# Turning token tiles in the second model: scaled tiles and a transpose, or one product with a diagonal

## The chip, the cores and the metric

The kernel runs on one core of a Trainium2 chip. The metric is the device time of one execution, in microseconds (us). A core has TensorE for matrix products (its records are PE, its weight loads PEld), VectorE (DVE), ScalarE (ACT) and GpSimd (POOL), which run side by side and wait for one another by semaphores; SyncE (SP) issues most transfers.

## The reference

Two models run one after the other on 256 tokens of width 1024. The change touches the second, of four blocks, whose core is this:

```python
def second_block(x, c, positions, ada_w, ada_b, norm_g, ffn_w1, ffn_w2, ...):
    for i in range(DEPTH_2):                                    # 4 blocks
        h = modulate_2(rms_norm_2(x, norm_g[i, 0]), sh_a, sc_a) # "norm"
        y = mixer(h)                        # i = 0, 3: mla; 1: stick_breaking; 2: retention
        x = x + g_a[:, None, :] * rms_norm_2(y, norm_g[i, 1])
        h = modulate_2(rms_norm_2(x, norm_g[i, 2]), sh_f, sc_f) # "fnorm"
        y = jnp.square(jax.nn.relu(h @ ffn_w1[i])) @ ffn_w2[i]
        x = x + g_f[:, None, :] * rms_norm_2(y, norm_g[i, 3])
    return x

def rms_norm_2(x, g):
    y = xf * lax.rsqrt(jnp.mean(xf * xf, axis=-1, keepdims=True) + EPS)
    return (y * g).astype(x.dtype)
```

So there are eight norms of the residual x, one ahead of each mixer and one ahead of each feed-forward stage (FFN). Everything is float32.

## The kernel before, in words

The residual x of the second model lies with tokens on the 128 partitions: two token tiles t = 0, 1, each 1024 wide, handled in halves of 512 (`h_tok(t, half)` in the tensor hT). The dense products want it the other way round, with the 1024 features on the partitions, in eight pieces k of 128. Between the two lies a **turn**, `turn_pe` (L1084): it both scales each token by its root 1/sqrt(mean square + eps) and transposes. There are eight turns, named b0_norm, b0_fnorm, and so on to b3_fnorm.

How a turn comes about:

- ScalarE squares the halves of x with a running sum (`square_act`, L959) and makes the root of a token tile from it by a logarithm and an exponential (`rms_act`, L967 and L970); VectorE supplies one small half sum to it (`half_dve`, L1019).
- VectorE writes, for each t, a 128x128 matrix with the roots on the diagonal: the identity times the column of roots (`diag_dve`, L1042).
- TensorE multiplies each 128x128 piece of x by this diagonal (L1094), 8 pieces for t = 0 and 8 for t = 1. The product is the transposed and scaled piece. Piece k goes to bank 4 + k // 2, at column 256 (k % 2) + 128 t, so a bank is full only when both token tiles are in it, and the banks fill in order during t = 1.
- ScalarE reads the banks with scale and bias of the modulation (`scaled_act`, L1132), 8 pieces of 128x256. In the blocks with an mla mixer (0 and 3) the norm turn is read by ScalarE for k = 0 to 3 and by VectorE for k = 4 to 7 (L2906).
- Except there, the pieces are split into a high and a low part, on VectorE (L1153, L1162) and ScalarE (L1142), and every weight tile of 1024 columns is split too, by ScalarE (L2427 in the FFN, L873 elsewhere) and VectorE (L3096, L877). TensorE then makes three products for each pair of pieces (L2032, L940; L2025 and L2028 in block 3). In the mla blocks TensorE multiplies the float32 pieces as they are (L1777).

The order on each engine is written out by hand. In the FFN of blocks 0 to 2 ScalarE has, behind the last root, two copies of a row from the banks (L1168, for the modulation of the next block), then the first weight tile (L2427), then L1132. In block 3 the two copies are missing; in the norm turns of blocks 1 and 2 the first weight tile is L873. VectorE has its half of the first weight tile (L3096 or L877) behind the diagonals. Ahead of the FFN, TensorE clears four banks (L1996) between the turn and the first product. At block 0 x comes from the first model through banks: TensorE transposes it (L2062), ScalarE squares it there and VectorE copies it to hT (L3146). GpSimd clears one area at the start of block 3 (L3228), as soon as the last half of x is there.

Of the kernel before, what the change touches and what calls it, by code (L numbers as in the profile page):

```python
# [19 lines left out]
ALU = mybir.AluOpType  # L20
# [3 lines left out]
P = 128  # L24
# [230 lines left out]
def block_program(nc, a, out, LAST=8):  # L255

    with ExitStack() as ctx:
# [376 lines left out]
        cond_row = region(W + 2048, [D])  # L634
        dots = small[:, 12:24]
        spill = region(18432 + 2560, [2, 512])
        diag = region(18432 + 3584, [TC, P])

        def two(v):
            return v.rearrange("p (a n) -> p a n", a=2)  # L640
# [2 lines left out]

            return hT[:, 4 * t + 2 * half:4 * t + 2 * half + 2, N:2 * N]

        def h_piece(t, k):
            return hT[:, 4 * t + k // 2, N + (k % 2) * P:N + (k % 2) * P + P]

        def gp_row(which, half):
            return uT[:, 4 * which + 2 * half:4 * which + 2 * half + 2, 0:N]  # L650
# [10 lines left out]

        def counters():
            return {"y_hi": 0, "sq": 0, "rs": 0, "u": 0, "t": 0, "sq_hist": [], "used": 0, "split": 0, "tok_sq": 0, "ms": 0,
                    "h_tok": 0, "diag": 0, "u_even": 0, "u_hi_act": 0, "u_hi_dve": 0}

        def stat_act(act, c, chunks, fill, width, rows=P):

# [312 lines left out]
        def h_square(act, c, half, t):  # L980
# [2 lines left out]
            act.wait_ge(S("h_tok"), c["h_tok"])  # L983
            square_act(act, c, h_tok(t, half), 16, half, t)

        def h_act(act, c):

            for half, t in BY_TOKENS:
                h_square(act, c, half, t)
                if half:  # L990
                    rms_act(act, c, 16, t)

        def down_act(act, c, name, norm):

            fs = [tok_fill(name, half, t) for half, t in BY_TOKENS]
            y_act(act, c, fs[0], 0, 0)
            y_act(act, c, fs[1], 1, 0)
            y_act(act, c, fs[2], 0, 1)
            if norm:
                h_square(act, c, 0, 0)  # L1000
                h_square(act, c, 1, 0)
            y_act(act, c, fs[3], 1, 1)
            if norm:
                rms_act(act, c, 16, 0)
                h_square(act, c, 0, 1)
                h_square(act, c, 1, 1)
                rms_act(act, c, 16, 1)

        def square_wait(dve, c, n=1):
            c["tok_sq"] += n  # L1010
            dve.wait_ge(S("tok_sq"), c["tok_sq"])

        def rms_wait(dve, c):
            c["ms"] += 1
            dve.wait_ge(S("tok_rs"), c["ms"])
# [19 lines left out]
                                           stat8[:, 12 + t:13 + t], h_tok(t, half), ALU.mult, ALU.add)\  # L1035
                .then_inc(S("h_tok"), 1)

        def diag_dve(dve, c):

            for t in range(TC):  # L1040
                rms_wait(dve, c)
                nc.vector.tensor_scalar(diag[:, t, :], ident, stat8[:, 28 + t:29 + t], None, ALU.mult)\  # L1042
                    .then_inc(S("diag"), 1)

        def post_dve(dve, c, i, which, name):

            rms_wait(dve, c)
            h_dve(dve, name, 0, 0)
            h_dve(dve, name, 1, 0)
            y_dve(dve, c, i, which, tok_fill(name, 1, 1), 1, 1)  # L1050
            rms_wait(dve, c)
            h_dve(dve, name, 0, 1)
            square_wait(dve, c)
            half_dve(16, 0)
            h_dve(dve, name, 1, 1)
            square_wait(dve, c, 2)
            half_dve(16, 1)
            c["tok_sq"] += 1
            diag_dve(dve, c)

        def down_dve(dve, c, i, name, norm, extra):

            y_dve(dve, c, i, 1, tok_fill(name, 0, 0), 0, 0)
            y_dve(dve, c, i, 1, tok_fill(name, 1, 0), 1, 0)
            rms_wait(dve, c)
            h_dve(dve, name, 0, 0)
            h_dve(dve, name, 1, 0)
            y_dve(dve, c, i, 1, tok_fill(name, 0, 1), 0, 1)
            if norm:
                extra()  # L1070
                square_wait(dve, c)
                half_dve(16, 0)
                c["tok_sq"] += 1
            y_dve(dve, c, i, 1, tok_fill(name, 1, 1), 1, 1)
            rms_wait(dve, c)
            h_dve(dve, name, 0, 1)
            h_dve(dve, name, 1, 1)
            if norm:
                square_wait(dve, c)
                half_dve(16, 1)  # L1080
                c["tok_sq"] += 1
                diag_dve(dve, c)

        def turn_pe(pe, c, name):  # L1084

            for t in range(TC):
                c["diag"] += 1
                pe.wait_ge(S("diag"), c["diag"])
                for k in range(KC):
                    f = plan[name][k // 2]  # L1090
                    o = (k % 2) * N + t * P
                    if t == 0 and k % 2 == 0:
                        f.open(pe)
                    mm = nc.tensor.matmul(PS[:, f.bank, o:o + P], h_piece(t, k), diag[:, t, :], start=True, stop=True)  # L1094
                    if t == TC - 1 and k % 2:
                        mm.then_inc(f.full.sem, 1)

        def cond_row_pe(pe, name):

# [975 lines left out]
        def _(act):  # L2075
# [377 lines left out]
            for half, t in BY_HALF:  # L2453
                f = tok_fill("entry", half, t)
                f.full.wait(act)
                square_act(act, c, PS[:, f.bank, :], 16, half, t)
                if half:
                    rms_act(act, c, 16, t)
            for i, kind in enumerate(KINDS):
                p = f"b{i}_"  # L2460
                if i:
# [18 lines left out]
        def _(dve):  # L2480
# [662 lines left out]
            for half, t in BY_HALF:  # L3143
# [2 lines left out]
                V_.tensor_copy(h_tok(t, half), two(PS[:, f.bank, :])).then_inc(f.free.sem, 1)  # L3146
                if half == 0:
                    half_dve(16, t)
            diag_dve(dve, c)
            for i, kind in enumerate(KINDS):  # L3150
                p = f"b{i}_"
                {"mla": mla_dve, "stick": stick_dve, "ret": ret_dve}[kind](i)
# [96 lines left out]
```

## Time and profile before

| what | value |
|---|---|
| device time, median of 3 runs | 2900.12 us (2898.72 to 2900.56) |
| profiled execution | span 2896.6 us, 3.5 us under the median for what lies around the span |
| busy: PE, PEld, DVE, ACT, POOL | 90%, 59%, 46%, 33%, 1% |
| chain that ended last | PE 72%, DMA 19%, DVE 4%, ACT 3%, issue 2% |
| mean granted clock of TensorE, 1500 us to the end | 0.97 of full |

The span is one profiled execution, from its first to its last instruction. The chain is followed back from the last instruction to what released it. The transfers of the chain belong to the experts of the first model, ahead of 1500 us. In the rows an arrow reads "written from": `banks<-arena,hT` writes the banks from arena and hT. "x32" counts records; a float32 product of 128x128 by 128x128 is two records, a transpose one. A time in brackets is the idle time ahead and who ended it. A granted clock of 1.00 is 2.4 GHz, 0.50 is 1.2 GHz.

### The profile page before, as it was taken

The numbers are of one execution on the slowest core, as the hardware profiler recorded it, in microseconds if no ns is written. First come the engines' busy times: TensorE is split into PE (matmuls) and PEld (weight loads), VectorE is DVE, ScalarE is ACT, GpSimd is POOL, SyncE is SP. The second block draws the span as 40 slices with busy tenths as digits, with TensorE's granted clock in tenths as the row PEclk, the third lists the DMA queues.
The fourth block names the chain that finished last, engine by engine and source line by source line (L and its number), as shares of the span: only waits on it lengthen the run. The fifth ranks groups of instructions, "written<-read, shape, count | busy, mean of one in ns | idle before, by whom it ended". The sixth has DMA issues, their size and how long they took to land.

```text
span 2896.6 us, 34037 instructions
## 1 busy us (share of the span) xinstructions
PE 2609.4 (90%) x13004; PEld 1714.1 (59%) x13004; DVE 1336.6 (46%) x2308; ACT 961.9 (33%) x1782; POOL 39.3 (1%) x51
## 2 busy tenths in 40 slices
PE   8999878787889888877779899999999999999999
PEld 3436423222465543222245789878988988985787
DVE  1764300001266520000025687567887458865676
ACT  3124210101121320000013555556555446544443
POOL 0010000000000000000000000000000000000000
PEclk9999999999999999999999999989999999999999
DMA  8674499999945459999991486515866427852242
GB/s 362 278 306 192 203 428 429 428 429 429 428 193 224 168 231 429 428 428 429 428 394 63 164 340 251 236 59 217 322 263 256 172 113 269 343 212 88 83 178 102
DMA packets 59492, 796.13 MB, mean 275 GB/s; under 512 B 8636, under 2 KB 9916, under 8 KB 10748
## 3 DMA queue, kind: packets, MB, share of 16 engines
q1 hardware_dynamic: 55664, 790.13, 66.8%
q10 hardware_dynamic: 3724, 4.59, 0.5%
q8 instruction: 68, 1.11, 0.2%
q14 instruction: 36, 0.29, 0.0%
HBM read 793.64 MB, written 1.05 MB: 274 GB/s over the span
## 4 chain that ended last, share of the span: by engine, by line
PE 72%; DMA 19%; DVE 4%; ACT 3%; issue 2%; SPq 0%; ACTq 0%; DVEq 0%; POOL 0%; POOLq 0%
PE banks L2008 12%; PE banks L2032 9%; PE banks L1504 8%; DMA ring<-in_t_gate 7%; PE banks L925 6%; DMA ring<-in_t_up 6%; PE banks L810 5%; PE banks L940 5%; DMA ring<-in_t_down 4%; PE banks L1520 3%; DMA arena<-in_t_gate 3%; PE banks L2025 2%; PE banks L1379 2%; PE banks L1573 2%; PE banks L797 2%
## 5 line engine op out<-in xcount | busy, mean ns | idle before, releaser
L1504 PE MATMUL banks<-ring,arena 128*64 128x512 f32 x1920 | 475.3, 619 | 100.9 <-DMA ring<-in_t_up 54.8
L1504 PEld LDWEIGHTS banks<-ring,arena 128*64 128x64 f32 x1920 | 162.3, 143 | 389.1 <-issue 345.4
L2633 DVE TENSOR_TENSOR arena<-arena,banks 128x512 f32<-128x512 f32 x32 | 22.0, 687 | 795.2 <-PE banks L1504 795.2
L3096 DVE TENSOR_TENSOR ring_lo<-ring,w_hi 128x1024 fp32r<-128x1024 f32 x256 | 313.3, 1225 | 133.9 <-ACT w_hi L2427 131.7
L2427 ACT CAST w_hi<-ring 128x1024 fp32r<-128x1024 f32 x256 | 268.4, 1055 | 314.9 <-PE banks L2008 166.3
L2032 PE MATMUL banks<-u_pair,w_hi 128*128 128x256 f32 x1536 | 278.8, 284 | 3.9 <-DVE ring_lo L3096 3.3
L2140 ACT COPY arena<-banks 32x512 f32 x96 | 55.3, 576 | 608.3 <-PE banks L1520 607.5
L2032 PEld LDWEIGHTS banks<-u_pair,w_hi 128*128 128x128 f32 x1536 | 240.1, 192 | 6.7 <-issue 3.9
L1520 PE MATMUL banks<-ring,arena 128*64 128x512 f32 x896 | 206.9, 616 | 28.4 <-DMA ring<-in_t_down 15.7
L2032 PE MATMUL banks<-u_pair,ring_lo 128*128 128x256 f32 x768 | 217.3, 283 | 0.0
L2008 PE MATMUL banks<-w_hi,ffn_h_hi 128*128 128x512 f32 x512 | 200.9, 392 | 0.0
L2008 PE MATMUL banks<-ring_lo,ffn_h_hi 128*128 128x512 f32 x512 | 199.4, 390 | 0.0
L2008 PE MATMUL banks<-w_hi,ffn_h_lo 128*128 128x512 f32 x512 | 199.3, 389 | 0.0
L1168 ACT COPY arena<-banks 128x256 f32<-128x256 f32 (+3 forms) x242 | 102.5, 443 | 231.0 <-PE banks L810 107.8
L3106 DVE SCALAR_TENSOR_TENSOR ring<-ring,arena 128x1024 f32<-128x1024 f32 x144 | 174.6, 1219 | 0.0
L1520 PEld LDWEIGHTS banks<-ring,arena 128*64 128x64 f32 x896 | 70.0, 141 | 147.3 <-issue 128.1
L2032 PEld LDWEIGHTS banks<-u_pair,ring_lo 128*128 128x128 f32 x768 | 147.3, 192 | 0.0
L810 PE MATMUL banks<-arena,ring 128*128 128x512 f32 (+1 forms) x384 | 140.4, 527 | 0.0
L810 PEld LDWEIGHTS banks<-arena,ring 128*128 128x128 f32 x384 | 73.7, 193 | 64.3 <-issue 60.6
L940 PE MATMUL banks<-uT_r,ring_lo 128*128 128x256 f32 x384 | 108.6, 283 | 0.0
L2008 PEld LDWEIGHTS banks<-w_hi,ffn_h_lo 128*128 128x128 f32 x512 | 96.1, 188 | 20.2
L2008 PEld LDWEIGHTS banks<-w_hi,ffn_h_hi 128*128 128x128 f32 x512 | 96.2, 188 | 19.9
(391 smaller groups left out, 4098.8 us busy)
## 6 DMA issues: line engine op xcount, KB each, us to landing
ring<-in_t_ffn SPq DMA_DIRECT2D x64, 2048.0 KB, 8.2
ring<-in_t_gate SPq DMA_DIRECT2D x60, 2048.0 KB, 22.0
ring<-in_t_up SPq DMA_DIRECT2D x60, 2048.0 KB, 22.1
ring<-in_t_down SPq DMA_DIRECT2D x56, 2048.0 KB, 21.6
ring<-in_t_ada_dots SPq DMA_DIRECT2D x48, 2048.0 KB, 9.7
ring<-in_t_ada SPq DMA_DIRECT2D x24, 2048.0 KB, 17.1
ring<-in_t_ret_in SPq DMA_DIRECT2D x12, 2048.0 KB, 8.2
arena<-in_t_down SPq DMA_DIRECT2D x8, 2048.0 KB, 31.3
```

What stands on the lines that cost most here:

```text
L797: mm = nc.tensor.matmul(PS[:, fs[m].bank, 0:width], w[:, q, m * P:(m + 1) * P], rhs(i, q), start=(q == 0), stop=(q == k - 1))
L810: mm = nc.tensor.matmul(PS[:, f.bank, 0:width], w[:, q, m * P:(m + 1) * P], rhs(i, q), start=(q == 0), stop=(q == k - 1))
L925: mm = nc.tensor.matmul(PS[:, f.bank, :], x[:, ts], w, start=(q.first and k == 0 and step == 0), stop=(q.last and k == 1 and step == 2))
L940: mm = nc.tensor.matmul(PS[:, f.bank, 0:N], w, x, start=(k == 0 and step == 0), stop=(k == KC - 1 and step == 2))
L1168: nc.scalar.copy(dst, src).then_inc(f.free.sem, 1)
L1504: mm = nc.tensor.matmul(PS[64 * h:64 * h + 64, f.bank, :], x_cur[:, b, k, :], wview(un[h0 + h], KC)[:, k, :], start=(k == 0), stop=(k == K ...
L1520: mm = nc.tensor.matmul(PS[64 * h:64 * h + 64, fd.bank, :], x_actT[:, b, fc % 4, (fc // 4) * 64:(fc // 4) * 64 + 64], wview(un[4 + fc // 4 ...
L2008: mm = nc.tensor.matmul(PS[:, down[2 * half + t].bank, :], x[:, t * P:(t + 1) * P], w[:, m, :], start=False, stop=False, skip_group_check= ...
L2032: mm = nc.tensor.matmul(PS[:, f.bank, 0:N], w[:, q, :], x[:, q, :], start=(q == 0 and x is u_hi and w is hi), stop=(q == KC - 1 and w is lo))
L2427: nc.scalar.copy(w_hi[:, n % 4], w).then_inc(S("ffn_w_hi"), 1)
L3096: TT(w_lo, w, w_hi[:, n % 4].bitcast(F32), ALU.subtract).then_inc(S("ffn_w_lo"), 1)
L3106: STT(w, w, 1.0, cond_row, ALU.mult, ALU.mult, accum_out=dots[:, n:n + 1]).then_inc(S("dot"), 1)
```

## The change

The diagonals are gone. In their place each half of a token tile is scaled by its column of roots into a new area `h_scaled`: both halves of t = 0 and half 0 of t = 1 on VectorE (`hs_dve`), half 1 of t = 1 on ScalarE (`hs_act`). TensorE then transposes the scaled pieces with the identity. It waits four times a turn, once for each half, instead of twice. The order of the pieces and banks stays.

```diff
@@ block_program
-        diag = region(18432 + 3584, [TC, P])
+        h_scaled = {"norm": region(W + 8192, [TC, D]), "fnorm": region(W, [TC, D])}
...
+        def hs_half(name, t, half):
+            return two(h_scaled[name][:, t, half * 512:half * 512 + 512])
...
+        def hs_act(act, c, name):
+            act.wait_ge(S("tok_rs"), c["ms"])
+            nc.scalar.activation(hs_half(name, 1, 1), h_tok(1, 1), ACT.Copy, scale=stat8[:, 29:30])\
+                .then_inc(S("hs_act"), 1)
...
         def h_act(act, c):
             for half, t in BY_TOKENS:
                 h_square(act, c, half, t)
                 if half:
                     rms_act(act, c, 16, t)
+            hs_act(act, c, "fnorm")
@@ down_act
                 h_square(act, c, 1, 1)
                 rms_act(act, c, 16, 1)
+                hs_act(act, c, "norm")
...
-        def diag_dve(dve, c):
-            for t in range(TC):
-                rms_wait(dve, c)
-                nc.vector.tensor_scalar(diag[:, t, :], ident, stat8[:, 28 + t:29 + t], None, ALU.mult)\
-                    .then_inc(S("diag"), 1)
+        def hs_dve(dve, c, name, t):
+            rms_wait(dve, c)
+            for half in range(TC - t):
+                nc.vector.tensor_scalar(hs_half(name, t, half), h_tok(t, half), stat8[:, 28 + t:29 + t], None, ALU.mult)\
+                    .then_inc(S("hs_dve"), 1)
@@ post_dve
             h_dve(dve, name, 1, 1)
+            hs_dve(dve, c, "fnorm", 0)
             square_wait(dve, c, 2)
             half_dve(16, 1)
             c["tok_sq"] += 1
-            diag_dve(dve, c)
+            hs_dve(dve, c, "fnorm", 1)
@@ down_dve
             if norm:
+                hs_dve(dve, c, "norm", 0)
                 square_wait(dve, c)
                 half_dve(16, 1)
                 c["tok_sq"] += 1
-                diag_dve(dve, c)
+                hs_dve(dve, c, "norm", 1)
@@ turn_pe
             for t in range(TC):
-                c["diag"] += 1
-                pe.wait_ge(S("diag"), c["diag"])
-                for k in range(KC):
...
-                    mm = nc.tensor.matmul(PS[:, f.bank, o:o + P], h_piece(t, k), diag[:, t, :], start=True, stop=True)
+                for half in range(2):
+                    by = "hs_act" if t and half else "hs_dve"
+                    c[by] += 1
+                    pe.wait_ge(S(by), c[by])
+                    for k in range(4 * half, 4 * half + 4):
...
+                        mm = nc.tensor.transpose(PS[:, f.bank, o:o + P], h_scaled[kind][:, t, k * P:(k + 1) * P], ident)
@@ scalar, entry of block 0
+            tok_fill("entry", 1, 1).free.wait(act)
+            hs_act(act, c, "norm")
@@ vector, entry of block 0
-            diag_dve(dve, c)
+            for t in range(TC):
+                for half in range(TC - t):
+                    tok_fill("entry", half, t).free.wait(dve)
+                hs_dve(dve, c, "norm", t)
```

VectorE at the fnorm turn of block 0, before (L1034 writes a half of x, L1019 is the half sum, L1042 the diagonals, L3096 the first weight tile, L1153 the first piece of the split; `tok_rs` is the root, `tok_sq` a finished square):

```order
L1034 SCALAR_TENSOR_TENSOR hT<-arena,stat,hT 128x2x256 [waits bank_free1,tok_rs]
L1019 TENSOR_SCALAR stat<-stat 128x1 [waits tok_sq]
L1034 SCALAR_TENSOR_TENSOR hT<-arena,stat,hT 128x2x256 [waits bank_free3]
L1019 TENSOR_SCALAR stat<-stat 128x1 [waits tok_sq]
L1042 TENSOR_SCALAR arena<-base,stat 128x128 [waits tok_rs] x2
L3096 TENSOR_TENSOR ring_lo_49<-ring,w_hi 128x8x128 [waits ffn_w_hi]
L1153 CAST u_pair<-arena 128x256 [waits u_even]
```

And with the change, where L1043, L1028, L1051, L3112 and L1167 stand for L1034, L1019, the scalings, L3096 and L1153:

```order
L1043 SCALAR_TENSOR_TENSOR hT<-arena,stat,hT 128x2x256 [waits bank_free1,tok_rs]
L1028 TENSOR_SCALAR stat<-stat 128x1 [waits tok_sq]
L1043 SCALAR_TENSOR_TENSOR hT<-arena,stat,hT 128x2x256 [waits bank_free3]
L1051 TENSOR_SCALAR arena<-hT,stat 128x512 [waits tok_rs]
L1051 TENSOR_SCALAR arena<-hT,stat 128x512
L1028 TENSOR_SCALAR stat<-stat 128x1 [waits tok_sq]
L1051 TENSOR_SCALAR arena<-hT,stat 128x512 [waits tok_rs]
L3112 TENSOR_TENSOR ring_lo_49<-ring,w_hi 128x8x128 [waits ffn_w_hi]
L1167 CAST u_pair<-arena 128x256 [waits u_even]
```

The two scalings of t = 0 now stand ahead of the half sum of t = 1 (the second L1028), and one scaling of t = 1 behind it.

ScalarE at the same place, before (L967 and L970 make the root of t = 1):

```order
L967 ACTIVATE stat<-stat 128x1 [waits tok_sq,ms_half]
L970 ACTIVATE stat<-stat 128x1 [waits tok_ln]
L1168 COPY arena<-banks 128x512 [waits bank_full0]
L1168 COPY arena<-banks 128x512 [waits bank_full1]
L2427 CAST w_hi<-ring 128x1024 [waits landed0]
L1132 ACTIVATE arena<-banks,MOD,AM 128x256 [waits bank_full4]
```

And with the change (L968 and L971 make the root, L990 is the scaling, L1182, L2441 and L1146 stand for L1168, L2427 and L1132):

```order
L968 ACTIVATE stat<-stat 128x1 [waits tok_sq,ms_half]
L971 ACTIVATE stat<-stat 128x1 [waits tok_ln]
L990 ACTIVATE arena<-hT,stat 128x512 [waits tok_rs]
L1182 COPY arena<-banks 128x512 [waits bank_full0]
L1182 COPY arena<-banks 128x512 [waits bank_full1]
L2441 CAST w_hi<-ring 128x1024 [waits landed0]
L1146 ACTIVATE arena<-banks,MOD,AM 128x256 [waits bank_full4]
```

One instruction of 128x512 comes in between the root and all that is queued behind it.

TensorE at the first turn, from bank 6 on, before:

```order
L1094 MATMUL banks<-arena,hT 128x128 [waits bank_free6]
L1094 MATMUL banks<-arena,hT 128x128
L1094 MATMUL banks<-arena,hT 128x128 [waits bank_free7]
L1094 MATMUL banks<-arena,hT 128x128
L1094 MATMUL banks<-arena,hT 128x128 [waits diag]
L1094 MATMUL banks<-arena,hT 128x128 x7
```

And with the change:

```order
L1108 MATMUL banks<-base,arena 128x128 [waits bank_free6,hs_dve]
L1108 MATMUL banks<-base,arena 128x128
L1108 MATMUL banks<-base,arena 128x128 [waits bank_free7]
L1108 MATMUL banks<-base,arena 128x128
L1108 MATMUL banks<-base,arena 128x128 [waits hs_dve]
L1108 MATMUL banks<-base,arena 128x128 x3
L1108 MATMUL banks<-base,arena 128x128 [waits hs_act]
L1108 MATMUL banks<-base,arena 128x128 x3
```

The pieces keep their order; t = 1 waits twice, and its first four pieces, which fill banks 4 and 5, need only VectorE.

## Rows read from the trace of the kernel before

**Rows 1.** Chain and waits, from 1500 us; waits: us, times, longest us.
```profile
by line: PE banks L2008 25.0%; PE banks L2032 19.2%; PE banks L925 12.4%; PE banks L940 9.5%; PE banks L2025 4.2%; PE banks L1094 2.8%; PE banks L1799 2.5%; issue 2.1%; PE banks L2028 2.1%; ACT arena L1132 1.6%; PE banks L1863 1.1%; PE bank
...
PE banks L1094 <- DVE arena L1042: 29.0, 8, 4.4
```

**Rows 2.** Chain of waits, from 1500 us, around the turns: start us, us, what.
```profile
1512.38 6.01 PE banks L1094 x28
...
1518.42 1.90 DVE arena L2906 x4
...
1635.15 4.65 PE banks L1094 x20
1639.83 3.76 ACT arena L1132 x8
...
1646.83 20.41 PE banks L2032 x168
...
1827.79 4.05 PE banks L1094 x20
1831.86 3.76 ACT arena L1132 x8
...
1985.75 4.00 PE banks L1094 x20
1989.78 3.75 ACT arena L1132 x8
...
2177.74 4.65 PE banks L1094 x20
2182.41 3.76 ACT arena L1132 x8
...
2587.65 6.40 PE banks L1094 x32
2594.05 13.96 PE banks L1777 x64
...
2703.87 4.65 PE banks L1094 x20
2708.55 3.76 ACT arena L1132 x8
```

**Rows 3.** Timeline of TensorE in four places: start us, us, engine, line.
```profile
988.31 0.74 PE L1729 MATMUL banks<-base,arena 128*128 128x128 f32 x3
...
1630.62 1.03 PE L1103 MATMUL banks<-base,cond 128*128 128x128 f32 x8
1635.15 6.49 PE L1094 MATMUL banks<-arena,hT 128*128 128x128 f32 x32 [3.50 <-DVE arena L1042]
...
1838.78 0.39 PE L940 MATMUL banks<-uT_r,st_in_w 128*128 128x256 f32 x1 [1.02 <-DVE ring_lo L877]
```

**Rows 4.** By stretch: busy of PE, PEld, DVE, ACT, POOL; granted clock; DMA; GB/s.
```profile
1635.10:1639.10 4.00, 3.95 (x18) 3.95 (x19) 1.50 (x2) 2.63 (x7) 0.00 (x0) 0.50 0.99 422
1827.80:1833.40 5.60, 5.46 (x32) 5.26 (x32) 2.29 (x5) 3.19 (x9) 0.00 (x0) 0.70 0.99 423
...
1907.00:1923.90 16.90, 16.90 (x48) 12.66 (x48) 11.85 (x25) 9.43 (x17) 0.00 (x0) 0.50 0.51 216
```

**Rows 5.** Timeline of ScalarE at the fnorm turn of block 0.
```profile
1635.75 0.20 ACT L970 ACTIVATE stat<-stat 128x1 f32<-128x1 f32 x1
1635.86 1.05 ACT L1168 COPY arena<-banks 128x512 f32<-128x512 f32 x2
1636.80 1.06 ACT L2427 CAST w_hi<-ring 128x1024 fp32r<-128x1024 f32 x1
```

**Rows 6.** VectorE: timeline before that turn, and lines (ns min/median/max).
```profile
1633.46 0.74 DVE L1034 SCALAR_TENSOR_TENSOR hT<-arena,stat,hT 128x512 f32<-128x512 f32 x1
...
L1042 DVE TENSOR_SCALAR arena<-base,stat x16: 275/284/891, 1512.1 to 2704.7; 128x128 f32<-128x128 f32 x16
...
L2645 DVE TENSOR_SCALAR y_hi<-arena,stat x12: 742/746/754, 677.1 to 1499.9; 128x1024 fp32r<-128x1024 f32 x12
```

More of the change, by code:

```diff
@@ L644, in h_tok @@
             return hT[:, 4 * t + 2 * half:4 * t + 2 * half + 2, N:2 * N]
-        def h_piece(t, k):
-            return hT[:, 4 * t + k // 2, N + (k % 2) * P:N + (k % 2) * P + P]
+        def hs_half(name, t, half):
+            return two(h_scaled[name][:, t, half * 512:half * 512 + 512])
         def gp_row(which, half):
@@ L663, in counters @@
             return {"y_hi": 0, "sq": 0, "rs": 0, "u": 0, "t": 0, "sq_hist": [], "used": 0, "split": 0, "tok_sq": 0, "ms": 0,
-                    "h_tok": 0, "diag": 0, "u_even": 0, "u_hi_act": 0, "u_hi_dve": 0}
+                    "h_tok": 0, "hs_dve": 0, "hs_act": 0, "u_even": 0, "u_hi_act": 0, "u_hi_dve": 0}
         def stat_act(act, c, chunks, fill, width, rows=P):
@@ L1081, in down_dve @@
                 c["tok_sq"] += 1
-                diag_dve(dve, c)
+                hs_dve(dve, c, "norm", 1)
         def turn_pe(pe, c, name):
+            kind = name.split("_")[1]
             for t in range(TC):
-                c["diag"] += 1
-                pe.wait_ge(S("diag"), c["diag"])
-                for k in range(KC):
[L1090 to L1093, printed above, removed]
-                    mm = nc.tensor.matmul(PS[:, f.bank, o:o + P], h_piece(t, k), diag[:, t, :], start=True, stop=True)
-                    if t == TC - 1 and k % 2:
-                        mm.then_inc(f.full.sem, 1)
+                for half in range(2):
[3 more added lines that the diff above has]
+                    for k in range(4 * half, 4 * half + 4):
+                        f = plan[name][k // 2]
+                        o = (k % 2) * N + t * P
+                        if t == 0 and k % 2 == 0:
+                            f.open(pe)
+                        mm = nc.tensor.transpose(PS[:, f.bank, o:o + P], h_scaled[kind][:, t, k * P:(k + 1) * P], ident)
+                        if t == TC - 1 and k % 2:
+                            mm.then_inc(f.full.sem, 1)
         def cond_row_pe(pe, name):
```

## The prediction

> **What bounds the kernel now.** I read the chain of waits first, cut to the second model (from 1500 us), because the change touches nothing earlier. Its head [rows 1] says that the diagonal matmuls of line 1094 hold 2.8% of 1396.6 us of path, 39 us, and the waits beside it that TensorE stood idle eight times before them, 29.0 us together. Its pieces [rows 2] show why: there are eight turns (two per block), and each lies on the path: VectorE or ScalarE ends a root, TensorE turns 16 tiles, ScalarE reads the banks (L1132), VectorE splits, and only then do the dense matmuls run unbroken (L2032 from 1646.83). Around a turn the path is serial; inside the dense stretches TensorE is the bound and nothing moves. So I need eight small sums, each on the instruction that really releases the next dense stretch.
>
> Next I read one turn as TensorE's timeline [rows 3] and the granted clock [rows 4]. A diagonal matmul is two records. In 1635.10 to 1639.10 there are 18 records in 4.00 us at a granted clock of 0.50, the 1.2 GHz level: 0.21 us each, 0.43 a matmul. TensorE had stood idle for 3.50 us before. This turn takes 6.49 us in all; of its 31 steps some 26 are at 0.21 and the rest at 0.11, so half clock held for about 5.6 us. In 1827.80 to 1833.40 the mean is 0.70, which is 3.4 us at half.
>
> **The change, part by part.**
>
> *TensorE, one transpose instead of one diagonal matmul.* A transpose is one record: eight of L1103 take 1.03 us at full clock, about 0.27 of it the tail of the last, so 0.11 us each. Three of L1729 take 0.74 us at clock 0.50 [rows 3]; with a tail of 0.27 to 0.42 that is 0.16 to 0.24 each, and I take 0.21, twice 0.11, as for the diagonal. A turn is then 16 x 0.21 = 3.4 us of work instead of up to 6.5.
> The Trainium skill ("TensorE: Matmul & The Clock Gate", Terms) says transpose mode is 4x faster for FP32; these rows show 2x (0.11 against 0.22), and the measurement decides. By the 4x the two transposes that the first bank waits for would cost 0.2 us less, 1.6 us over eight turns.
>
> *VectorE, a scaling of 128x512 instead of a 128x128 diagonal.* The trace has no such shape with a column of scalars. L2645 does 1024 columns in 0.746 us, L1042 does 128 in 0.28 [rows 6]; between them 512 costs 0.48, and about 0.42 from start to start. VectorE does three: both halves of t=0 and half 0 of t=1.
>
> *ScalarE, half 1 of t=1.* Its nearest row is the bank copy L1168, two 128x512 in 1.05 us [rows 5]: 0.52 from start to start, 0.6 alone. It enters ScalarE's queue right behind the root, so everything there moves by 0.52: L1168 (three blocks), the weight cast L2427 or L873 (1.03), then L1132.
>
> *Turn of block 0's fnorm in full.* The first half is scaled right after L1034, which ends at 1634.20, not after L1019; TensorE starts at 1634.67 instead of 1635.15. The t=0 tiles end near 1636.4. The root of t=1 ends at 1635.95; VectorE's half is done at 1636.46; the first bank is full at 1636.5 + 0.21 + 0.42 = 1637.15, instead of about 1639.8. ScalarE is not ready then: 1635.97 + 0.52 (new) + 1.0 (L1168) + 1.0 (L2427) = 1638.45. Now ScalarE is the last, and L1132 starts 1.4 us earlier instead of 2.7. Behind it lie 3.76 us of L1132, the casts, the next weight cast, and L2032 at 1646.83; VectorE's cast is held by its own L3096 until 1639.7, still 0.7 earlier than today, and its 3.8 us of split end in time. Gain 1.4.
>
> *The others by the same steps* [rows 2] (the root of t=1 ends 1635.95 - 1635.15 = 0.80 us after the turn's first matmul, and I take that for all but the norm turn of block 3):
> - fnorm of blocks 1 and 2: there the clock came back early, L1132 starts 4.03 us after the turn (block 2: 4.16), ScalarE allows 0.80 + 0.02 + 0.52 + 1.0 + 1.0 = 3.3. Gain 0.8 each.
> - fnorm of block 3: no L1168; ScalarE is free at 2706.25, against 2708.55. Gain 2.3.
> - norm of block 1: root 1828.6, plus 0.1 since L1019 now stands behind two scalings, + 0.52 + 1.03 = 1830.25 against 1831.86. Gain 1.6. Norm of block 2: 2180.2 against 2182.41, 2.2.
> - norm of block 0: what ends last is VectorE's L2906 at 1518.42, which waits for bank 6, the 14th tile: 1512.58 + 14 x 0.21 + 0.3 = 1515.8. Gain 2.6. The rope tables of VectorE follow and hide L1777.
> - norm of block 3: L1777 follows L1094 at once (2594.05), so TensorE's own time is on the path. The diagonal of t=0 took 0.89 us here instead of 0.28 [rows 6]; I charge the same 0.6 stall to the scaling, and L1019 behind it delays the root of t=1 by 0.7. First bank at about 2590.0, two L1132 (1.03), L1777 at 2591.1. Gain 2.8.
> Sum: 2.6 + 1.4 + 1.6 + 0.8 + 2.2 + 0.8 + 2.8 + 2.3 = 14.5 us.
>
> *What is late next: the clock.* Today the clock comes back 3.4 to 5.6 us after the half level began, still within the turn, so the dense tiles run at full clock (168 records of L2032 in 20.41 us, 0.12 each) [rows 2]. With light, gapped transposes the clock may come back only that long after the first dense matmul. The first weight tile is then 24 matmuls x 0.21 = 5.1 us. It starts about 1 us earlier than today, needs some 4 us today, paced by VectorE's split, and then waits 1.02 us for the second tile's weights [rows 3]; the second tile will be ready 0.8 to 2.3 us earlier. Between a clock that comes back on time (0) and one late by 3.4 us (1.7 us where TensorE is the bound), I take 0.3 for each of the fnorm turns, 0.4 and 0.5 for norms 1 and 2. Norm 0 is covered by VectorE. Norm 3 has no cover: L1777 would run 2 to 5.4 us at half speed, 1.0 to 2.7; I take 1.9. Sum 4.0.
> The Trainium skill ("TensorE: Matmul & The Clock Gate", Part 4) says a transpose doesn't count as busy for the clock gate. No row here isolates that. By the rule the losses go by their upper values and the gain falls to about 8 us; without it the loss is near 1.5 and the gain 13.
>
> **Sum.** 14.5 - 4.0 = 10.5 us on the profiled execution (span 2896.6; the median run is 2900.1, 3.5 above, for what lies around it). I carry the difference to the median: 2889.6 us.
>
> **Rivals.**
> *A, the clock gives most of it back.* The dense tile at half clock overruns the ready time in all seven uncovered turns. For it: TensorE idles before every turn, up to 4.4 us [rows 1]. Against: full-size matmuls at clock 0.50 got it back in 3.4 and 5.6 us [rows 3, 4]. Price 7 x 1.3 to 1.7, about 10 us of the 14.5; the gain is 4, giving 2896.
> *B, slower: the clock stays at half for long.* In 1907.00 to 1923.90 the engine showed 16.90 of 16.90 us busy and the clock stayed at 0.50 [rows 4]: so busy small work alone does not always bring it back. If after the transposes half clock lasts beyond the first dense tile, each further tile costs 24 x (0.21 - 0.12) = 2.2 us. Eight turns gain 14.5; the point of break-even is about one tile plus the lost slack in each. Two such tiles a turn give 7 x (4.4 + 0.5) - 14.5 = +20, one and a half +12: from 2902 on. Against: the short matmuls there are not the dense tiles of L2032, whose stretches stand at 1.00 throughout.
> *C, no change, hidden anyway.* If ScalarE's extra 0.5 and VectorE's longer ops delayed the path, that is, the turn never was last. Against: TensorE's L1094 pieces stand in the chain in all eight [rows 2], and L1132 waits for it. Left of it is the case that ScalarE-bound turns gain only 0 to 0.5: 14.5 falls to about 9 before the clock, 5 after: 2895.
> *D, it doesn't do what it says:* a transpose of scaled tiles as slow as the diagonal. Then ScalarE and TensorE tie and the time is 2900. L1103's 0.11 speaks against; 2%.
>
> **How the numbers follow.** Forecast 0.60 (2885 to 2894), A 0.18, B 0.07, C 0.09, D 0.02, and 0.04 for a gain above 15 us. 0.2% is 5.8 us, about what a measurement tells from no change: faster is below 2894.3. Forecast and the large gain give 0.64, of A and C (centres 2896, 2895) I count 0.10: faster 0.74. Same: the rest of A and C, D, and a third of B: 0.21. Slower 0.05. The range leaves out B and the largest gains: 2884.5 to 2897.5.
>
> **What would show it.** Right: the transposes at 0.21 us each, a turn of about 4 us from first to last instead of 5.3 to 6.5; the first L1132 of a fnorm turn directly behind L2427 with no wait for TensorE; L1132 1 to 2 us earlier after each turn's root; L1777 of block 3 about 3 us after the turn's start instead of 6.4. The clock step: half clock reaching into the first L2032 or L940 tile, and the wait before the second tile (1.0 us now) shrinking. Wrong: half clock still granted in the second dense tile of a turn (B), a new ScalarE wait on the path longer than 0.6 us, or a scaling over 0.75 us.

## The result and the profile after

The changed kernel takes 2883.89 us (median of 4 runs, 2881.29 to 2885.30), the kernel before 2900.28 us beside it: a ratio of 0.9946, 95% interval 0.9931 to 0.9960, or 16.4 us less. Forecast were 10.5 us less, with a range down to 2884.5. A second series on another occasion gave 2888.95 against 2897.64, so 8.7 us less by the medians. Its ratio is 0.9953 (0.9935 to 0.9971), which is 13.6 us, because its five times fall into two groups (2878.7 and 2880.5, and 2889.0 to 2891.9). Over both series the means differ by 13.9 us. The profiled execution spans 2879.3 us and is itself the fastest of its series, at 2881.29 us.

The chain and the waits after, in the columns of [rows 1]: the waits of the turn for VectorE fell only from 29.0 to 26.9 us, while ScalarE's waits for the turn (22.4 us in eight places before) are all but gone.

```profile
PE banks L1108 <- DVE arena L1051: 26.9, 9, 3.9
...
ACT arena L1146 <- PE banks L1108: 2.7, 2, 2.1
```

The chain of waits after, from 1500 us (start us, us, what), answering to [rows 2]:

```profile
1514.59 3.26 PE banks L1108 x14
1517.88 1.90 DVE arena L2922 x4
...
1634.76 0.72 ACT arena L990
1635.48 0.96 ACT arena L1182 x2
1636.44 0.94 ACT w_hi L2441
1637.38 3.66 ACT arena L1146 x8
...
1644.28 20.41 PE banks L2046 x168
...
1824.71 0.79 DVE arena L1051 x2
...
1826.79 1.04 ACT st_in_w L874
...
2573.21 1.12 PE banks L1108 x4
2574.36 1.97 PE banks L1108 x8
2576.32 15.02 PE banks L1791 x64
...
2689.63 0.72 ACT arena L990
2690.35 0.94 ACT w_hi L2441
2691.29 3.65 ACT arena L1146 x8
```

Where a turn of 20 to 32 matmuls stood in the chain, in the feed-forward turns there is now none: the path runs over ScalarE alone, root, scaling (L990), the two copies, the weight cast, the reading of the banks. L1146 begins 3.8 us after the turn's first transpose (1637.28 against 1633.46); forecast was 1638.45 - 1634.67 = 3.8. In the norm turns of blocks 1 and 2 the path runs over VectorE's two scalings of t = 0 (L1051), the root and the weight cast (L874). Only in the mla blocks is the turn still in the chain, for 3.3 and 3.1 us instead of 6.0 and 6.4.

TensorE at the fnorm turn of block 0, timeline as in [rows 3]:

```profile
1633.46 3.81 PE L1108 MATMUL banks<-base,arena 128*128 128x128 f32 x16 [3.03 <-DVE arena L1051]
1637.06 1.91 PE L2010 MATMUL banks<-zeros_bf 128*128 128x512 bf16 x4
```

3.81 us instead of 6.49 for the same 16 pieces, after a wait of 3.03 us instead of 3.50; the four clearing products of the FFN (L2010) follow at once. ScalarE's timeline there, as in [rows 5]:

```profile
1634.52 0.20 ACT L971 ACTIVATE stat<-stat 128x1 f32<-128x1 f32 x1
1634.76 0.72 ACT L990 ACTIVATE arena<-hT,stat 128x512 f32<-128x512 f32 x1
1635.39 1.05 ACT L1182 COPY arena<-banks 128x512 f32<-128x512 f32 x2
1636.33 1.05 ACT L2441 CAST w_hi<-ring 128x1024 fp32r<-128x1024 f32 x1
1637.28 3.77 ACT L1146 ACTIVATE arena<-banks,MOD,AM 128x256 f32<-128x256 f32 x8
```

The durations of the new operations (ns, min/median/max), answering to the line of L1042 in [rows 6]:

```profile
L1051 DVE TENSOR_SCALAR arena<-hT,stat x24: 478/484/1253, 1514.1 to 2689.6; 128x512 f32<-128x512 f32 x24
```

```profile
L990 ACT ACTIVATE arena<-hT,stat x8: 722/722/723, 1514.2 to 2689.6; 128x512 f32<-128x512 f32 x8
```

**Where the time went.** I cut each trace at the starts of the same records into stretches. "Turn stretches" are the ones that hold a turn, from the last product of the stage before to a point in the dense work after it; "stick" is the attention of block 1, which no changed line touches; the lengths are my subtraction of record starts, in us.

| profiled execution | entry | FFN 0, 1, 2 | FFN 3 | norm 1 | norm 2 | norm 3 | sum of turn stretches | stick | span |
|---|---|---|---|---|---|---|---|---|---|
| before | 32.59 | 193.68, 193.04, 193.18 | 191.64 | 79.56 | 216.12 | 28.47 | 1128.3 | 52.60 | 2896.6 |
| before, again | 29.46 | 191.62, 193.68, 193.69 | 191.64 | 80.16 | 215.41 | 27.58 | 1123.2 | 54.55 | 2897.4 |
| changed | 29.10 | 192.36 (all three) | 189.38 | 77.95 | 214.00 | 26.72 | 1114.2 | 45.44 | 2879.3 |
| changed, again | 27.90 | 192.37, 192.38, 192.37 | 189.76 | 78.15 | 213.93 | 27.91 | 1114.8 | 52.74 | 2887.7 |

Of the 17.3 us between the first and the third row, 14.1 lie in the turn stretches and 7.2 in the stick stage; the first model took 2.0 us more and a dense stage of block 3, where 3.4 us at half clock fell, 1.6 more. The stick stage has the same instructions in both and another granted clock. By stretch, columns as in [rows 4], the kernel before and then the changed one:

```profile
1904.00:1956.20 52.20, 49.74 (x225) 37.04 (x224) 40.77 (x87) 31.42 (x66) 0.00 (x0) 0.84 0.21 81
```

```profile
1899.90:1944.90 45.00, 42.01 (x224) 31.58 (x225) 40.05 (x87) 31.41 (x66) 0.00 (x0) 1.00 0.24 94
```

The same instructions, 0.84 of the clock and 52 us, or full clock and 45 us. Whether the change had caused that was the first question.

### The profile page after: what moved, and what is told of

Same layout as the page of the kernel before. It is cut to its first block, busy times and chain, and to the rows that moved or that the text cites. A ratio compares the mean times of both kernels' runs of the same rounds, so it can differ in the third digit from the quotient of the medians.

```text
span 2879.3 us, 33808 instructions
## 1 busy us (share of the span) xinstructions
PE 2593.2 (90%) x12876; PEld 1691.1 (59%) x12876; DVE 1341.1 (47%) x2316; ACT 967.0 (34%) x1790; POOL 39.6 (1%) x51
## 4 chain that ended last, share of the span: by engine, by line
PE 71%; DMA 20%; DVE 4%; ACT 3%; issue 2%; SPq 0%; ACTq 0%; DVEq 0%; POOL 0%; POOLq 0%
PE banks L2022 12%; DMA ring<-in_t_gate 10%; PE banks L2046 9%; PE banks L1518 8%; PE banks L926 6%; PE banks L941 5%; PE banks L811 5%; DMA ring<-in_t_down 4%; DMA ring<-in_t_up 3%; DMA arena<-in_t_gate 3%; PE banks L1534 3%; PE banks L2039 2%; PE banks L1393 2%; PE banks L1587 2%; PE banks L798 1%
## 5 line engine op out<-in xcount | busy, mean ns | idle before, releaser
L3112 DVE TENSOR_TENSOR ring_lo<-ring,w_hi 128x1024 fp32r<-128x1024 f32 x256 | 313.3, 1225 | 136.2 <-ACT w_hi L2441 134.0
L2441 ACT CAST w_hi<-ring 128x1024 fp32r<-128x1024 f32 x256 | 268.5, 1056 | 315.0 <-PE banks L2022 166.4
L1182 ACT COPY arena<-banks 128x256 f32<-128x256 f32 (+3 forms) x242 | 102.5, 442 | 232.8 <-PE banks L811 106.2
```

What stands on the lines that cost most here:

```text
L1182: nc.scalar.copy(dst, src).then_inc(f.free.sem, 1)
L2441: nc.scalar.copy(w_hi[:, n % 4], w).then_inc(S("ffn_w_hi"), 1)
L3112: TT(w_lo, w, w_hi[:, n % 4].bitcast(F32), ALU.subtract).then_inc(S("ffn_w_lo"), 1)
```

## The experiments

### The kernel before, once more, and the changed kernel, once more

Edit: none in either.

> The kernel before, unchanged, run again for the stretch of block 1's stick mixer, which took 52.2 us at a mean granted clock of 0.84 in its profile and 45.0 us at 1.00 in the profile of the changed kernel. Theory L (a matter of luck: where the clock's state falls in this stage differs from run to run): in this profile or in the spread of the times the stage is seen both ways, and the runs of the kernel before spread over about 7 us. Theory S (the stage falls to half clock in every run of the kernel before): mean clock again near 0.84 over the stage, 52 us, and all runs within 2 us of 2900.

Measured: 2899.19 us (2896.53 to 2901.36, 10 runs), ratio 0.9996 (0.9987 to 1.0006). The profile of it, by stretch:

```profile
1633.80:1637.70 3.90, 3.90 (x34) 3.77 (x35) 1.49 (x3) 3.78 (x10) 0.00 (x0) 1.00 0.98 420
1905.20:1925.70 20.50, 20.34 (x58) 14.90 (x58) 13.24 (x28) 10.14 (x19) 0.00 (x0) 0.50 0.37 157
```

The stick stage fell to half clock as in the first profile. But the fnorm turn of block 0, at 0.50 in [rows 4], ran at 1.00 here: the diagonal matmuls took 3.84 us, and FFN 0 only 191.62 us. So neither theory holds whole: the fall in the stick stage is usual, and the clock of single turns, on which my terms rested, differs from one execution to the next.

> The changed kernel, unchanged, for a second profile and more times. From one profile each of before and after, the stretches with a turn in them account for 10 to 14 us and the stick mixer of block 1 for 7 to 9 us more (45.4 us against 52.6 and 54.6). Theory L (the stick stage keeps full clock in some runs by luck, in any of the kernels): this profile shows about 52 us there in at least one more run of the changed kernel, the times spread by several us, and the median stays at 2883 to 2887, since the turns alone give 12 to 14. Rival K (the change keeps the stick stage at full clock): 45.4 us again, all times within 2 us of 2883.

Measured: 2888.95 us (2878.70 to 2891.89, 5 runs). The profile by stretch:

```profile
1897.50:1949.90 52.40, 49.83 (x225) 37.11 (x226) 40.88 (x88) 31.53 (x66) 0.00 (x0) 0.84 0.20 81
1900.70:1917.80 17.10, 16.98 (x48) 12.64 (x47) 11.58 (x24) 9.25 (x17) 0.00 (x0) 0.50 0.49 209
```

The same changed kernel falls too, and its turn stretches repeat to 0.6 us (1114.2 and 1114.8). The full clock of the stick stage in the first profile was an accident of that execution, not the work of the change. The nine times of the changed kernel together have their median at 2884.66 us and spread over 13 us.

### Is it the transpose, or the earlier start?

```diff
 # on the changed kernel
-                        mm = nc.tensor.transpose(PS[...], h_scaled[kind][...], ident)
+                        mm = nc.tensor.matmul(PS[...], h_scaled[kind][...], ident, start=True, stop=True)
```

> The changed kernel with a plain product with the identity (two records each) in place of each transpose; the scalings stay where they are. Theory T (TensorE's shorter turn is what was gained): a turn on TensorE takes 5.3 to 6.5 us again and about 10 us of the gain go: 2892 to 2897, with block 0's L1777 stage hidden, norm of block 3 back by about 3 us. Rival P (the gain comes from the earlier start of t=0 and the order of the scalings, TensorE's speed is hidden): within 2 us of the changed kernel, 2882 to 2886.

Measured: 2892.24 us (2889.24 to 2899.67, 10 runs), ratio 0.9981 (0.9970 to 0.9991). Scaling first and then multiplying by the identity keeps 7.8 us of gain over the kernel before by the medians (2900.06 us in that series), about half of what the change gave in the first series; its ten times fall into two groups (2889 to 2893 and 2897 to 2900), and by the ratio only 5.5 us are kept. The turn stretches sum to 1120.0, 5.4 us above the changed kernel. What was lost lies where TensorE is the last: entry 31.10, norm 2 216.05, FFN 3 190.39. The feed-forward stretches of blocks 0 to 2 hardly moved (192.37 to 192.70), though their turns were two records a piece again. Two of the eight turns (fnorm of block 0, norm of block 1) happened to run at full clock in this profile, in 3.9 us, so it shows too little of the loss. The median lies in theory T's range, the turn stretches lost half of what T said, and the norm of block 3 (27.00) did not go back by 3 us. The converse:

```diff
 # on the kernel before; the diagonals are still made and waited for, but the scaling is left out
-                    mm = nc.tensor.matmul(PS[...], h_piece(t, k), diag[:, t, :], start=True, stop=True)
+                    mm = nc.tensor.transpose(PS[...], h_piece(t, k), ident)
```

> The kernel before, with its diagonals still made and waited for, but each piece of x transposed with the identity instead of multiplied by the diagonal. It leaves out the scaling by the root. Theory T (TensorE's shorter turn is the whole gain of the change and scaling on VectorE and ScalarE costs what it saves): the FFN stretches of blocks 0 to 2 take 191.6 us as with all scaling on VectorE, since ScalarE's 0.72 us is absent, 2882 to 2885. Rival E (the earlier start of t=0, 0.48 us in each fnorm turn, is on the path too): FFN stretches 192.1 or more and 2886 to 2889.

Measured: 2880.10 us (2875.57 to 2882.75, 4 runs), ratio 0.9939 (0.9924 to 0.9954); turn stretches 1110.3. With VectorE and ScalarE as they were before, half the instructions on TensorE give 15.5 us against the mean of the two profiles of before (1125.8), all that the change gives and the price of its scalings on top: FFN 0 to 2 are at 191.61, as in the next kernel, where TensorE starts 0.48 us earlier. With one record a piece the earlier start adds nothing there.

### What the scaling on ScalarE costs

All four halves on VectorE:

```diff
-            hs_act(act, c, "fnorm")
...
-            for half in range(TC - t):
+            for half in range(2):
...
-                    by = "hs_act" if t and half else "hs_dve"
+                    by = "hs_dve"
```

> The changed kernel with half 1 of t=1 scaled on VectorE too; ScalarE's 0.72 us instruction is gone. Theory A (ScalarE's queue of root, scaling, bank copies and weight cast is now last in the four fnorm turns and the norm turns of blocks 1 and 2): 0.5 to 0.7 us less in each of the six, 3 to 4 us in all, 2879 to 2881. Rival B (the banks or VectorE's own queue are last): VectorE's 0.42 us more delays its weight part L3112 and nothing is gained, or up to 2.5 us are lost.

Measured: 2883.50 us (2880.08 to 2889.41, 4 runs), ratio 0.9952 (0.9936 to 0.9969), from which nothing can be told: its stick stage fell to 52.7 us. The profile tells it. The chain at the fnorm turn of block 0:

```profile
1631.94 0.20 ACT stat L971
1632.14 0.96 ACT arena L1180 x2
1633.10 0.95 ACT w_hi L2439
1634.04 3.66 ACT arena L1144 x8
```

The copy now follows the root directly; in the chain after, 0.72 us of L990 stand between. FFN 0, 1 and 2 are 191.61, 191.62, 191.61 instead of 192.36, so 0.75 less in each, and the turn stretches sum to 1111.3. That is 3.2 less than the mean of the changed kernel's two profiles. ScalarE was indeed the last in these three, and a scaling on VectorE, which had a slot free, costs nothing there. In the other three stretches named by theory A only 0.1 (FFN 3), 0.2 and 0.3 us (norms 1 and 2) came, where 0.5 to 0.7 were expected; why is open.

### The clearing on GpSimd beside the scaling

In the norm turn of block 3 two scalings took far more than 2 x 0.48. VectorE and GpSimd of the changed kernel, timelines:

```profile
2571.51 1.65 DVE L1051 TENSOR_SCALAR arena<-hT,stat 128x512 f32<-128x512 f32 x2
```

```profile
2571.65 1.23 POOL L3247 MEMSET arena<- 128x1024 f32 x1 [1060.67 <-DVE hT L1043]
```

```diff
-                        pool.wait_ge(S("h_tok"), 4 * 2 * i)
+                        pool.wait_ge(S("hs_dve"), 3 * (2 * i + 1))
                     nc.gpsimd.memset(ml_pT, 0.0).then_inc(S("pT_zero"), 1)
```

> The changed kernel with GpSimd's clearing of an area in block 3 held until VectorE's scalings of that turn are done. Theory G (the scaling that took 1.25 us instead of 0.48 in the norm turn of block 3 was blocked by GpSimd's 1.2 us instruction that ran at the same time): all scalings at 0.48, L1108's first transpose 0 to 0.1 us earlier but t=1's root 0.7 us earlier, and the first read of the banks 0.7 us sooner after the turn's start than 3.10. Rival: the long scaling has another cause and stays at 1.2 us.

Measured, one run: 2884.17 us, from which alone nothing can be told. The same two lines in its timelines:

```profile
2578.50 0.88 DVE L1051 TENSOR_SCALAR arena<-hT,stat 128x512 f32<-128x512 f32 x2
```

```profile
2580.58 0.95 POOL L3247 MEMSET arena<- 128x1024 f32 x1 [1070.66 <-DVE arena L1051]
```

0.88 instead of 1.65 us, a clearing of 0.95 instead of 1.23, and a norm stretch of 25.84 instead of 26.72 and 27.91. The two instructions held each other up while they overlapped; the stall of the scalings is 0.77 us, where I had charged 0.6. Part of the shorter stretch is clock. The last kernel below has the late clearing and differs in this stretch from the kernel with zeros ahead of the turns by that alone, both at full clock: 24.85 against 25.62, again 0.77. The Trainium skill ("SBUF — State Buffer", Who interferes with whom) says that a scaling of this kind can take a pair of ports shared with GpSimd, and that the second to start is blocked entirely; the second scaling, 1.253 us long and begun inside the clearing, agrees in the main. It ended 0.27 us after the clearing, sooner than the 0.484 it takes alone.

### Holding the clock through the wait

If the turn is dear because it runs at half clock after 3 to 4 us of idling, products of zeros in that idle time should buy what the change buys. On the kernel with all scalings on VectorE, and on the kernel before:

```diff
 # turn_pe, ahead of the loop over t
+            plan[name][0].open(pe)
+            for _ in range(12):
+                nc.tensor.matmul(PS[:, plan[name][0].bank, :], zeros_bf[:, :], zero_row, start=True, stop=True,
+                                 skip_group_check=True)
```

> All scaling on VectorE, and 12 products of zeros (bf16, 128x512, into the bank that the turn overwrites) on TensorE in the idle time ahead of each turn. Theory H (the half clock of the turns comes from the idle ahead of them and costs something in what follows): the turns run at the granted clock 1.00, 16 transposes in 1.8 us of work, b3's norm and the following L1777 stage gain 1 to 2 us, the rest 0 to 0.5 each: 2879 to 2882. Rival Z (products of zeros don't hold the clock, or TensorE's clock is hidden behind ScalarE and VectorE): turns still at 0.5 or no gain: 2883 to 2885, or slower if the 12 products (2.6 us, 5.1 at half clock) run past the first scaling.

Measured: 2883.62 us (2880.98 to 2885.95, 4 runs), ratio 0.9951 (0.9936 to 0.9966), no better than without the products (2883.50). TensorE's timeline:

```profile
1626.84 2.75 PE L1098 MATMUL banks<-zeros_bf 128*128 128x512 bf16 x12
1630.03 1.09 PE L1110 MATMUL banks<-base,arena 128*128 128x128 f32 x8 [0.43 <-DVE arena L1049]
1631.87 1.09 PE L1110 MATMUL banks<-base,arena 128*128 128x128 f32 x8 [0.75 <-DVE arena L1049]
```

The step worked, eight transposes in 1.09 us, and the turn stretches fell from 1111.3 to 1108.4. By stretch that is 1.5 us at the entry, 0.6 each in FFN 3 and the norm of block 3, 0.3 and 0.1 in norms 1 and 2, and nothing in FFN 0 to 2. In the profile the 3.0 us were used up by stages that the edit doesn't touch: 2.3 more in the first model, 1.6 more each in a dense stage of block 1 and one of block 3, and 1.7 less in block 0.

> The kernel before, diagonals and all, with 12 products of zeros (bf16, 128x512) on TensorE in the idle time ahead of each turn. Theory C (what the turns of the kernel before cost too much is the half clock after the idle time, and much of the change's gain is that it cares less about it): turns of 3.8 us instead of 5.3 to 6.6 in all eight places, the three FFN stretches near 191.6 us as in the one turn that happened to run at full clock, the stretches with turns 10 to 14 us shorter in sum, 2885 to 2890. Rival R (the number of records and the waits for the diagonals count, not the clock): stretches as before within 3 us, 2897 to 2900.

Measured: 2881.99 us (2879.02 to 2884.06, 5 runs), ratio 0.9943 (0.9929 to 0.9956). TensorE's timeline of it:

```profile
1625.90 2.75 PE L1088 MATMUL banks<-zeros_bf 128*128 128x512 bf16 x12
1629.56 3.84 PE L1098 MATMUL banks<-arena,hT 128*128 128x128 f32 x32 [0.91 <-DVE arena L1042]
```

All eight turns of this kernel took 3.7 to 3.84 us (6.49 in [rows 3]), FFN 0 to 2 are 191.62, the turn stretches 1111.9. Twelve products of zeros a turn gain as much as the change does, with diagonals and without any scaling. The two kernels with zeros differ by 3.5 us in their turn stretches (1111.9 and 1108.4); without zeros, diagonals (1125.8) and transposes with all scalings on VectorE (1111.3) differ by 14.5. So about three quarters of what the transposes save is the price of the half clock. At full clock the diagonal turn, 3.84 us, is already hidden in the feed-forward turns of blocks 0 to 2, and there the changed kernel is 0.75 us a turn slower than this one.

### Holding the clock in the stick stage

```diff
 # stick stage of the changed kernel, into the bank of its first output
+                keep(4)
                 for f in plan[p + "qk"][-4:] + plan[p + "v"][-2:]:
...
                 for s in range(16 + 6):
+                    if s in (2, 3, 4):
+                        keep(3)
```

> The changed kernel with 13 products of zeros on TensorE in the first waits of block 1's stick mixer. Theory L (the stage falls to half clock by luck, when a stretch with its first idle gaps is light enough, and then needs 14 to 20 us to come back; that is 7 us of spread that has nothing to do with the change): granted clock 1.00 through the stage, 45 to 46 us in the profile, median 5 to 7 us under the changed kernel's 2884 to 2888, and a narrower spread. Rival Z: products of zeros don't keep the clock here, 52 us as in most runs.

Measured: 2880.56 us (2875.78 to 2882.84, 5 runs), ratio 0.9935 (0.9921 to 0.9949). By stretch:

```profile
1899.20:1945.00 45.80, 44.87 (x242) 33.06 (x241) 40.69 (x89) 31.75 (x66) 0.00 (x0) 1.00 0.23 93
```

46.14 us at full clock instead of 52 to 55. The median lies 4.1 us under that of the changed kernel's nine times, and the spread is 7.0 us instead of 13: theory L, if a little less than it said.

> All together: scaling on VectorE alone, GpSimd's clearing after the scalings of block 3's norm turn, products of zeros ahead of each turn and in the first waits of the stick mixer. If the parts add up from their profiles (turn stretches 1105 us instead of 1114 to 1115, one more us from the late clearing, stick 45.5 instead of 52.5 in most runs): 2870 to 2876. If TensorE's clock elsewhere or the transfers' order take it back: 2878 to 2884.

All of it together (scalings on VectorE, late clearing, zeros ahead of turns and in the stick stage): 2873.50 us (2870.88 to 2874.30, 4 runs), ratio 0.9913 (0.9898 to 0.9928). It beats both kernels, its median is in the range expected, and its times lie within 3.4 us. Turn stretches 1107.4 and stick 46.15 us; against the means of the two profiles of before (1125.8 and 53.6) that is 18.4 + 7.4 = 25.8 us, and the medians differ by 25.9.

## Why the prediction was right, and where not

The mechanism held, and its size in sum: the turn stretches went from a mean of 1125.8 to 1114.5, 11.3 us less, where 14.5 - 4.0 = 10.5 were forecast. Against the one profile of before that the forecast was worked out from, they fell by 14.1. By term, measured between the means of the two profiles of each kernel:

- **Norm of block 0**: forecast 2.6, measured 2.5. VectorE's L2922 starts 3.3 us after the turn, as worked out (3.2).
- **fnorm of blocks 0, 1, 2**: forecast 1.4, 0.8, 0.8 less 0.3 each, so 2.1 in all; measured 2.3 in all (193.15 to 192.37 each). That ScalarE is last, with no wait for TensorE, is in the chain. I had its scaling at 0.6 us alone; it takes 0.722.
- **fnorm of block 3**: forecast 2.3 - 0.3, measured 2.1.
- **Norms 1 and 2**: forecast 1.6 - 0.4 and 2.2 - 0.5, measured 1.8 and 1.8.
- **Norm of block 3**: forecast 2.8 - 1.9 = 0.9, measured 0.7. The stall beside the clearing was nearly as charged, and without it the stretch gains 0.77 more. The mark "L1777 about 3 us after the turn's start" failed: it came after 4.25 us (2576.30 against 2572.05). The turn had itself begun 0.7 us earlier; counted from the last product of the stage before, these products begin after 7.9 instead of 10.6 us, 2.7 less, where 2.8 were forecast.
- **Unit prices**: the scaling on VectorE was taken at 0.48 us and took 0.484; the transpose at 0.21 at half clock, and sixteen with their gaps took 3.81.

**The clock term** was right in sum by two errors that cancelled. The step itself came. In both profiles of the kernel before, the first dense products behind every turn ran at full clock. In both of the changed kernel the half clock reached into the first dense tile of norms 1 and 2 and into the float32 products behind the norm of block 3. The first profile of the changed kernel by stretch, inside the first dense tile of norms 1 and 2:

```profile
1829.97:1833.90 3.93, 3.93 (x18) 3.93 (x19) 3.44 (x11) 3.93 (x9) 0.00 (x0) 0.50 1.03 442
2171.90:2175.20 3.30, 3.30 (x17) 3.20 (x16) 2.81 (x7) 2.88 (x6) 0.00 (x0) 0.50 1.07 457
```

And the products behind the norm of block 3, timelines of before, changed, and changed again:

```profile
2593.89 14.12 PE L1777 MATMUL banks<-arena,ring 128*128 128x256 f32 x64
```

```profile
2576.30 15.04 PE L1791 MATMUL banks<-arena,ring 128*128 128x256 f32 x64
```

```profile
2582.67 16.23 PE L1791 MATMUL banks<-arena,ring 128*128 128x256 f32 x64
```

The first error is its price. Behind the norm of block 3 it was 0.9 and 2.1 us, where I had charged 1.9. In norms 1 and 2 (0.4 and 0.5 charged) it cost nothing: the wait for the second tile's weights, 1.02 us in [rows 3], took it up, and in the first of these profiles the second tile follows without a wait, 4.7 and 4.8 us after the first. With all scalings on VectorE no half clock fell on that tile in block 1, and the second tile began 5.1 us after the first, behind a wait of 1.01 us. In FFN 0 to 2 (0.9 charged) it cost nothing either: 192.36 us are the 191.61 of the kernel with the scalings on VectorE and the 0.75 of the scaling. At the entry I had called it covered, and the kernels without and with zeros differ there by 1.5 us. The half clock did not always outlast the turn. The changed kernel by stretch, at the fnorm turn of block 1 (transposes only in the first row) and behind it:

```profile
1973.90:1977.30 3.40, 3.33 (x15) 3.06 (x16) 0.96 (x4) 3.24 (x10) 0.00 (x0) 0.50 1.02 439
1977.40:1984.80 7.40, 4.72 (x31) 3.47 (x29) 6.37 (x16) 7.40 (x15) 0.00 (x0) 1.00 0.59 248
```

Here the clock rose from the 1.2 GHz to the 2.4 GHz level while TensorE had done nothing but transposes since its idle time; its next work, L2010, begins at 1977.44 us. The Trainium skill ("TensorE: Matmul & The Clock Gate", Part 4) says that transposes don't count as busy for the gate in the same way; here they did, and the gain of about 8 us that I worked out from it did not come. The second error is that the gross gains themselves hung on the clock: the turn of before at full clock costs less than I read from its one profile, as its second profile and the kernel with zeros show.

**What the forecast lacked** is the stick stage, and with it lies the most likely reason why the first median fell 0.6 us below the range. Its half clock stood in my own evidence (16.90 us busy at 0.50 [rows 4]), and I used it only to argue rival B. It falls to half clock, for 14 to 20 us, in nine of the ten profiles without zeros in that stage; the tenth is that of the changed kernel's first series, and that execution was 7 us shorter for it. The times of the changed kernel spread over 13 us, and I had taken one profile of the kernel before as if it were the kernel. The excess of the first series over the 11.3 us is of the size of such an accident; why all four of its runs were low is not settled, since only one was profiled.

**The rivals.** A (the clock gives most back) and B (half clock in later dense tiles) did not come: directly behind the turns no dense tile after the first stands at half clock. C named the right thing, ScalarE as the last engine, and the kernels with the scaling moved off it put its price at 0.75 us in each of three turns, not at the gain. D is excluded by the 3.81 us. The mark I gave for the second tile's wait (1.0 us, shrinking) came in norms 1 and 2, where it is gone; in the FFNs it stands at 1.09 us as before, and in FFN 0 to 2 no half clock reached the tile.

## What to carry to other kernels

In this kernel TensorE mostly ran a short serial job at half clock when it had idled for 3 to 4 us before. Halving the job's instructions helps, but so do a dozen products of zeros in the wait, so price the two against each other before work is moved to other engines. Whether the zeros also steady the times is not shown: the kernel with zeros in both places spread over 3.4 us, but in four runs. When a job moves to an engine, look at what is queued behind it there: in three feed-forward turns the same scaling was free on VectorE (0.48 us) and on the path on ScalarE (0.72 us). And profile the kernel before twice: a term read from one execution's clock is a draw, and a stretch that no edit touches may be the largest difference between two profiles.

## What the runs showed of the hardware

- Short matmuls in the stick stage kept the half clock for 14 to 20 us while the records show TensorE busy without a gap (16.98 of 17.10 us in the second profile of the changed kernel). Thirteen products of zeros in the stage's first waits prevented it in both kernels profiled with them. Why the fall comes in most executions and not in all stays open.
- Idle gaps of 3 to 4 us ahead of a turn mostly, not always, led to the half clock: in the second profile of before two of eight turns ran at full clock, 3.84 us, where the other fourteen of its two profiles took 5.3 to 6.8. In the second profile of the changed kernel the first turn did, 16 transposes in 1.97 us.
- A float32 transpose costs about half of a float32 product of the same shape at full clock: 16 in 1.97 us against 16 products (32 records) in 3.84.
- A half clock that falls on a tile with a wait behind it can cost nothing: 3.4 us or more of it in the first tile of norms 1 and 2 used up a wait of 1.0 us, while behind the norm of block 3, with no wait, it cost 0.9 and 2.1 us.
- The time of FFN 0, 1 or 2 depends on the turn ahead of it only through what is last: 191.62 us with a diagonal turn at full clock, 191.61 with scalings on VectorE, 192.36 with one on ScalarE, 193.0 to 193.7 with a diagonal turn that ran wholly or partly at half clock.
